# Gate tiles of the input projection moved from the branch stage in between the pieces of attention

## The chip, the cores and the metric

One core of one Trainium2 chip runs one program. The metric is the device time in microseconds; every number is for both layers and both token streams together. The program has one launch and no host arithmetic.

## The reference, cut to what matters

Two layers, one after the other, act on 1024 latent tokens and 128 prompt tokens (1152 in all, width 1024). In each, `h` is a modulated RMS norm of `x`, and one projection `h @ w_in` feeds three mixers and all their gates:

- the first is two gated long convolutions (by transforms), `y_hy`; the second differential attention in 4 heads, `y_at`; the third pooling, `y_pl`;
- each `y` is multiplied by `silu(z)` of its own 512 columns of the projection;
- `merged = sum over branches of sigmoid(mg_b) * (y_b @ w_b_o)`, `mg_b` being 1024 further columns each;
- `x + gate * (merged @ w_out)` is the next `x`.

Attention: per head two maps of queries and keys, `softmax` of each, `pr0 - lam * pr1`, times the values, then an RMS norm over the 128 value columns. Latent queries see 1024 latent and 256 cached keys, prompt queries the 128 prompt keys.

## The kernel before, in words

All tensors are held with channels (or tokens, for probabilities) on the 128 partitions. A product in fp32 is made of three in a rounded format: each operand is split into a rounded high part and a remainder, `hh`/`hl` for `h` and `wh`/`wl` for a weight tile. ScalarE rounds (`high`), GpSimd or VectorE subtracts (`low`), and TensorE forms high x high, high x low and low x high. A tile of 128 output columns over the 1152 tokens is 8 rows (k) x 3 products x 3 chunks of 384 columns, 72 matmuls; a branch product has 4 rows, 36 matmuls (`project`, line 120 on, whose matmul is L127).

The stages of a layer, each closed by a barrier, are: the filter network and spectra, `modulated_norm`, `mixers_in` (24 tiles of the projection), `values`, `long_conv` twice, `attention`, `branches_out`, `output`. The norm stores `hh` and `hl` to DRAM (`h_keep`, L612 and L614), since the convolutions need the room, and attention's ScalarE queue loads them again (4608 KB each). `values` loads `v` (2304 KB, L1055) for the first convolution, whose folds (L1323) start at once.

`attention` (L1394 on) runs 4 heads of 9 units: 8 blocks of 128 latent queries and one of prompt queries. Per unit, the two maps of scores (L1547) lie in two sets of three banks; VectorE takes the largest (L1840), ScalarE the exponential (L1683) and the scaling of the second map (L1690), GpSimd adds the maps (L1778); TensorE transposes the result in three fills of one bank (L1570), each of which ScalarE rounds (L1699) and VectorE takes the remainder of (L1860) before the next fill; every two units follow the product with the values (L1587), the sums of squares (L1596) and the spread of the root (L1604). The order in each engine's queue is written out by hand, unit u+1's scores between unit u-1's transposes.

`branches_out` (L1927 on) makes, for each of 3 branches, 4 gate tiles (12 in all, silu, L2041), splits `y * silu(z)` (L2083, L2046, L2085), and then 8 times a gate tile (24 in all, sigmoid, L2027) followed by a product of 4 rows, which VectorE multiplies by the gate (L2092) and adds to `merged` (L2097). The 36 gate tiles are those that the change moves. Weights come over SP's queue (L1959, L1963) into two buffers, are rounded by ScalarE (L2021) and subtracted by GpSimd (L2061), two tiles ahead:

```python
with pe.Fori(0, KD // 2) as i:
    for b in range(2):
...
        project(pe, chunks(banks(0)), wh[:, b], wl[:, b], hh, hl, KD).then_inc(S["g"], 1)
...
        project(pe, chunks(banks(1)), wh[:, b, KD:KO], wl[:, b, KD:KO], yh, yl, CT
                ).then_inc(S["z"], 1)
```

## Time and profile before

| | |
|---|---|
| median of 3 runs | 4578.84 us (4577.19 to 4579.85) |
| profiled execution, its span | 4593.8 us |
| mean granted TensorE clock | 0.886 |
| TensorE busy | 3727.9 us, 81% |
| VectorE, ScalarE, GpSimd busy | 36%, 27%, 26% |
| DMA | 428.99 MB, mean 93 GB/s |

The span is from the first to the last instruction of one profiled execution; the profile lists no other time for it. Times of an execution are in us from its start. A granted clock of 1.00 is 2.4 GHz, of 0.50 is 1.2 GHz. PE is TensorE, PEld its weight loads, DVE VectorE, ACT ScalarE, POOL GpSimd, SPq the queue of SyncE that issues DMAs.

### The profile page before, as it was taken

How to read it: one execution, taken by the hardware profiler on the slowest of the kernel's cores; microseconds unless marked ns; L12 is line 12 of the kernel's file. 1: busy time of each engine (PE TensorE's matmuls, PEld its weight loads, DVE VectorE, ACT ScalarE, POOL GpSimd, SP SyncE). 2: the span in 40 equal slices, each digit the busy share in tenths (PEclk: the TensorE clock that was granted, in tenths of full speed). 3: DMA queues.
4: the chain of work that ended last, by engine and by line, in shares of the span. 5: the costliest groups of instructions: out<-in, count | busy, mean ns of one | idle time of the engine just before them, and what ended most of it. 6: DMA issues, size and time to landing. Idle time of an engine off the chain costs nothing. (4 is left out here: it accounts for less than half of the span.)

```text
span 4593.8 us, 53336 instructions
## 1 busy us (share of the span) xinstructions
PE 3727.9 (81%) x19468; PEld 3375.5 (73%) x19468; DVE 1665.4 (36%) x1950; ACT 1256.8 (27%) x1848; POOL 1175.2 (26%) x542
## 2 busy tenths in 40 slices
PE   3874999787577799999938849997875777999998
PEld 2664988565466699999926649885664567999998
DVE  4234323254666412121242343232546664121212
ACT  2232122122455412121122321221224563121211
POOL 2011121054343222212120121210543342212211
PEclk8877999888787899999968779998887888999999
DMA  2544211234511111110415442122445111111104
GB/s 85 185 132 182 87 64 71 93 128 160 173 36 45 46 54 65 34 68 30 141 54 185 135 180 87 63 78 88 134 157 167 37 44 53 51 62 37 64 32 149
DMA packets 156156, 428.99 MB, mean 93 GB/s; under 512 B 30202, under 2 KB 51966, under 8 KB 154688
## 3 DMA queue, kind: packets, MB, share of 16 engines
q1 hardware_dynamic: 139936, 379.55, 24.8%
q10 hardware_dynamic: 16128, 48.26, 2.9%
q8 instruction: 52, 0.85, 0.1%
q14 instruction: 40, 0.33, 0.0%
HBM read 312.38 MB, written 120.08 MB: 94 GB/s over the span
## 5 line engine op out<-in xcount | busy, mean ns | idle before, releaser
L2061 POOL TENSOR_TENSOR branch_wl<-branch_raw,branch_wh 128x1536 fp32r<-128x1536 f32 (+1 forms) x72 | 267.3, 3713 | 926.5 <-ACT branch_wh L2021 926.5
L127 PE MATMUL ps<-hh,branch_wh 128*128 128x384 f32 x1728 | 398.2, 338 | 41.2 <-POOL branch_wl L2061 24.2
L127 PE MATMUL ps<-hl,branch_wh 128*128 128x384 f32 x1728 | 396.2, 337 | 0.0
L127 PE MATMUL ps<-hh,branch_wl 128*128 128x384 f32 x1728 | 396.1, 337 | 0.0
L127 PEld LDWEIGHTS ps<-hh,branch_wh 128*128 128x128 f32 x1728 | 311.5, 190 | 44.5 <-issue 44.5
L2092 DVE TENSOR_TENSOR branch_gate<-ps,branch_gate 128x1152 f32<-128x1152 f32 x48 | 65.2, 1358 | 751.8 <-PE ps L127 751.8
L127 PEld LDWEIGHTS ps<-hl,branch_wh 128*128 128x128 f32 x1728 | 311.9, 190 | 0.0
L127 PEld LDWEIGHTS ps<-hh,branch_wl 128*128 128x128 f32 x1728 | 311.5, 190 | 0.0
L1292 POOL TENSOR_TENSOR conv_dl<-conv_draw,conv_dh 128x512 fp32r<-128x512 f32 x128 | 180.2, 1415 | 471.4 <-ACT conv_dh L1242 470.6
L1778 POOL TENSOR_TENSOR attn_prob<-attn_prob 128x1280 f32<-128x1280 f32 (+1 forms) x72 | 190.4, 2644 | 241.1 <-ACT attn_prob L1690 241.1
L127 PE MATMUL ps<-hh,mixin_wh 128*128 128x384 f32 x720 | 167.2, 340 | 102.2 <-POOL mixin_wl L943 97.0
L1840 DVE TENSOR_REDUCE attn_nmax<-ps 128x1 f32<-128x1280 f32 x144 | 194.7, 1353 | 43.9 <-PE ps L1547 43.7
L127 PEld LDWEIGHTS ps<-hh,mixin_wh 128*128 128x128 f32 x720 | 130.4, 191 | 106.6 <-issue 98.2
L1570 PE MATMUL ps<-ident,attn_prob 128*128 128x128 f32 x648 | 125.6, 313 | 101.1 <-DVE attn_wl L1860 100.6
L943 POOL TENSOR_TENSOR mixin_wl<-w_in_raw,mixin_wh 128x1024 fp32r<-128x1024 f32 x48 | 114.7, 2392 | 350.9 <-ACT mixin_wh L868 350.9
L2021 ACT CAST branch_wh<-branch_raw 128x1536 fp32r<-128x1536 f32 (+1 forms) x72 | 96.2, 1339 | 382.2 <-PE ps L127 382.1
L2027 ACT ACTIVATE branch_gate<-ps 128x1152 f32<-128x1152 f32 x48 | 54.5, 1135 | 524.8 <-PE ps L127 524.8
L1683 ACT ACTIVATE attn_prob<-ps,attn_nmax 128x1280 f32<-128x1280 f32 x144 | 176.1, 1223 | 68.3 <-DVE attn_nmax L1840 63.9
L868 ACT CAST mixin_wh<-w_in_raw 128x1024 fp32r<-128x1024 f32 x48 | 50.2, 1049 | 489.2 <-DMA w_in_raw<-in_w_in 371.2
L1570 PEld LDWEIGHTS ps<-ident,attn_prob 128*128 128x128 f32 x648 | 83.5, 159 | 127.4 <-DVE attn_wl L1860 93.6
L1547 PE MATMUL ps<-attn_kh,attn_qs 128*128 128x512 f32 (+2 forms) x400 | 133.6, 446 | 44.7 <-DVE attn_kl L1832 34.7
L127 PE MATMUL ps<-hl,mixin_wh 128*128 128x384 f32 x720 | 165.9, 338 | 0.0
(262 smaller groups left out, 8421.2 us busy)
## 6 DMA issues: line engine op xcount, KB each, us to landing
branch_raw<-in_w_mo SPq DMA_DIRECT2D x48, 768.0 KB, 4.2
H_dram<-fspec_hout ACTq DMA_DIRECT2D x100, 256.0 KB
fspec_araw<-in_w_ada SPq DMA_DIRECT2D x48, 512.0 KB, 4.6
conv_hs<-H_dram SPq DMA_DIRECT2D x32, 768.0 KB, 4.5
w_in_raw<-in_w_in SPq DMA_DIRECT2D x44, 512.0 KB, 3.8
fspec_draw<-in_dft_taps SPq DMA_DIRECT2D x68, 256.0 KB, 3.0
conv_draw<-in_dft_fwd SPq DMA_DIRECT2D x64, 256.0 KB, 2.6
conv_draw<-in_dft_inv SPq DMA_DIRECT2D x64, 256.0 KB, 2.6
```

Source lines behind the costliest of these rows:

```text
L127: last = pe.matmul(out, w[:, k, :], x[:, k, cols], start=(k == 0 and n == 0), stop=(k == kt - 1 and n == 2))
L943: pool.tensor_tensor(wl[:, b], raw[:, b], wh[:, b].bitcast(F32), ALU.subtract).then_inc(S["lo"], 1)
L1292: pool.tensor_tensor(dl[:, b], draw[:, b], dh[:, b].bitcast(F32), ALU.subtract).then_inc(S["lo"], 1)
L1547: last = pe.matmul(flat[:, 1536 * c + at:1536 * c + at + width], qs[:, c, q0:q0 + P], keys[:, c, k0 + at:k0 + at + width], start=(m == 0), ...
L1570: last = pe.transpose(ps[:, 6, q * P:(q + 1) * P], prob0[:, u % 3, (at + q) * P:(at + q + 1) * P], ident[:])
L1683: nc.scalar.activation(dst[:, 0:n], flat[:, 1536 * c:1536 * c + n], ACT.Exp, bias=nmax[:, c:c + 1], accum_out=total[:, u % 2, c:c + 1]).th ...
L1778: pool.tensor_tensor(prob0[:, u % 3, 0:n], prob0[:, u % 3, 0:n], prob1[:, u % 2, 0:n], ALU.add).then_inc(S["w"], 1)
L1840: dve.tensor_reduce(nmax[:, c:c + 1], flat[:, 1536 * c:1536 * c + n], AX_X, ALU.max, negate=True).then_inc(S["max"], 1)
L2021: nc.scalar.copy(wh[:, b, 0:size], raw[:, b, 0:size]).then_inc(S["hi"], 1)
L2027: nc.scalar.activation(three(gate[:, b]), banks(0)[:, :, 0:CH], ACT.Sigmoid).then_inc(S["sig"], 1)
L2061: pool.tensor_tensor(wl[:, b, 0:size], raw[:, b, 0:size], wh[:, b, 0:size].bitcast(F32), ALU.subtract).then_inc(S["lo"], 1)
L2092: dve.tensor_tensor(three(gate[:, b]), banks(1)[:, :, 0:CH], three(gate[:, b]), ALU.mult).then_inc(S["p"], 1)
```

## The change

The norm no longer stores `h`. Attention follows `values` directly, so `hh` and `hl` stay in place, and the convolutions come after it. `attention_and_gates` has 36 steps and 4 that drain; step n makes one gate tile, its 8 rows laid between the pieces of unit n (scores) and unit n-2 (transposes). The scores of both maps now share one set of three banks, `gate_banks` is another set of three; the probabilities of the second map and the split weights of the product with the values have one buffer where they had two. Gate weights come in half tiles (256 KB) into a ring of 3; ScalarE copies each finished tile out of its banks (`gate_out`), and SP stores it to `gates` in DRAM (576 KB), unactivated. The loops over heads are unrolled, as are those over the convolutions and the branches. `values` no longer loads `v`; the first convolution does, and waits for it. `branches_out` keeps only the 24 products: it loads each gate row (576 KB) and applies silu or sigmoid there, with weights (256 KB) in a ring of 3 and two buffers of gates; the first branch writes `merged` directly.

```diff
@@ build
             with ExitStack() as hctx:
...
-                raw = hctx.enter_context(nc.sbuf_tensor("w_in_raw", [P, 2, KD, P], F32))
-                modulated_norm(nc, A, l, ps, pr, mod, ones, x_state, hh, hl, raw, h_keep, s_kept)
-                wv = hctx.enter_context(nc.sbuf_tensor("w_v_raw", [P, KD, BR], F32))
-                mixers_in(nc, A, l, ps, pr, ident, hh, hl, raw, wv, mix, qk)
-                values(nc, A, O, l, ps, hh, hl, wv, mix, v, vrows, s_kept)
-            with nc.Fori(0, 2) as o:
-                long_conv(nc, A, l, o, ps, ident, v, mix, H_dram, Hp_dram, hinv)
-            vctx.close()
-            with ExitStack() as hctx:
-                hh = hctx.enter_context(nc.sbuf_tensor("hh2", [P, KD, NT], F32R))
-                hl = hctx.enter_context(nc.sbuf_tensor("hl2", [P, KD, NT], F32R))
-                attention(nc, A, O, l, ps, pr, ident, ones, qk, vrows, mix, hh, hl, h_keep)
...
-                branches_out(nc, A, l, ps, hh, hl, mix, merged, wo)
+                graw = hctx.enter_context(nc.sbuf_tensor("w_g_raw", [P, 3, KD // 2, P], F32))
+                with ExitStack() as wctx:
...
+                    values(nc, A, O, l, ps, hh, hl, wv, vrows, graw)
+                attention_and_gates(nc, A, O, l, ps, pr, ident, ones, qk, vrows, mix, gates, hh, hl, graw)
+            with ExitStack() as vctx:
...
+                for o in range(2):
+                    long_conv(nc, A, l, o, ps, ident, v, mix, H_dram, Hp_dram, hinv)
+            with ExitStack() as mctx:
...
+                branches_out(nc, A, l, ps, mix, gates, merged, wo)
@@ modulated_norm, sync
-                    sp.dma_start(h_keep[0, :, k], hh[:, k].bitcast(F32)).then_inc(s_kept, 16)
...
-                    sp.dma_start(h_keep[1, :, k], hl[:, k].bitcast(F32)).then_inc(s_kept, 16)
@@ values, sync
-                sp.dma_start(v[:], mix[2].rearrange("c p n -> p c n")).then_inc(s_hy, 16)
+                for j in range(3):
+                    sp.dma_start(graw[:, j], A["w_g"][l, j].rearrange("p (k c) -> p k c", c=P)).then_inc(s_gw, 16)
@@ long_conv, sync, then vector
+                if o == 0:
+                    sp.dma_start(v[:], mix[2].rearrange("c p n -> p c n")).then_inc(S["vin"], 16)
...
+                if o == 0:
+                    dve.wait_ge(S["vin"], 16)
@@ attention_and_gates, sync (step n is unit n = 9 h + u; NALL = 36, STEPS = 40)
+                for n in range(STEPS):
+                    if 1 <= n <= NALL:
+                        sp.wait_ge(S["gev"], n)
+                        sp.dma_start(gates[n - 1], stage[:]).then_inc(S["gst"], 16)
+                    gate_weights(2 * n + 5)
...
+                    gate_weights(2 * n + 6)
@@ tensor
+                def gate(n, *rows):
...
+                    for k in rows:
+                        if k == 0 and n:
+                            pe.wait_ge(S["gev"], n)
+                        j = 2 * n + k // HALF
+                        if k % HALF == 0:
+                            pe.wait_ge(S["glo"], j + 1)
+                        for m, (a, b) in enumerate(((gh, hh), (gh, hl), (gl, hh))):
+                            for c in range(3):
+                                last = pe.matmul(gate_banks[:, c, :], a[:, j % RING, k % HALF, :],
...
+                turn_cached(0)
+                turn_new(0)
+                for n in range(STEPS):
+                    if n == 0:
+                        gate(n, 0, 1, 2, 3)
+                    if n < NALL:
+                        scores(n, 0)
+                    gate(n, *((4, 5) if n == 0 else (0,)))
...
+                        spread(*got)
+                    if n:
+                        gate(n, 1)
+                    if got := due(n, WITH_V):
+                        with_v(*got)
...
+                        gate(n, 2)
+                    if n < NALL:
+                        scores(n, 1)
...
+                        turn(n - 2, 0)
+                    if n:
+                        gate(n, 3)
...
+                        sums(*got)
+                    if n:
+                        gate(n, 4)
+                    if len(turned) > 1:
+                        turn(n - 2, 1)
+                    if n:
+                        gate(n, 5)
+                    gate(n, 6)
+                    if len(turned) > 2:
+                        turn(n - 2, 2)
+                    gate(n, 7)
@@ scalar
+                for n in range(STEPS):
+                    if 1 <= n <= NALL:
+                        gate_out(n - 1)
+                        second_map(n - 1)
+                    if n < NALL:
+                        softmax(n, 0)
...
+                    gate_high(2 * n + 2)
+                    if got := due(n, WITH_V):
+                        take(*got)
...
+                        high(n - 2, 0)
+                    if n < NALL:
+                        softmax(n, 1)
+                    if len(turned) > 1:
+                        high(n - 2, 1)
+                    gate_high(2 * n + 3)
+                    if len(turned) > 2:
+                        high(n - 2, 2)
@@ branches_out, sync (NP = 24 products, q = 8 br + m; RING = 3)
+                def branch_in(br):
                     for t in range(CT):
+                        if br:
+                            sp.wait_ge(S["yl"], CT * (br - 1) + t + 1)
+                        sp.dma_start(z[:, t], gates[CT * br + t]).then_inc(s_z[t], 16)
+                        sp.dma_start(yin[:, t], mix[br + 4, t]).then_inc(s_z[t], 16)
+
+                def product_in(q):
+                    if q >= RING:
+                        sp.wait_ge(S["lo"], q - RING + 1)
+                    sp.dma_start(raw[:, q % RING], A["w_mo"][l, q // KD, q % KD]).then_inc(s_w[q % RING], 16)
+                    if q >= 2:
+                        sp.wait_ge(S["t"], q - 1)
+                    sp.dma_start(gate[:, q % 2], gates[N_BRANCH * CT + q]).then_inc(s_r[q % 2], 16)
+
+                branch_in(0)
+                for q in range(NP):
+                    product_in(q)
+                    if q % KD == 1 and q // KD + 1 < N_BRANCH:
+                        branch_in(q // KD + 1)
@@ tensor
+                for q in range(NP):
...
+                    pe.wait_ge(S["lo"], q + 1)
+                    if q >= 2:
+                        pe.wait_ge(S["p"], q - 1)
...
+                    project(pe, chunks(banks(q)), wh[:, q % RING], wl[:, q % RING], yh[:, br % 2], yl[:, br % 2], CT, ready
@@ scalar
+                silu(0)
+                for t in range(CT):
+                    round_y(0, t)
+                    if t < 2:
+                        high(t)
+                for q in range(NP):
+                    br, m = divmod(q, KD)
+                    high(q + 2)
+                    sigmoid(q)
+                    if br + 1 < N_BRANCH:
+                        if m == 2:
+                            silu(br + 1)
+                        elif 3 <= m < 3 + CT:
+                            round_y(br + 1, m - 3)
@@ vector
+                for q in range(NP):
+                    br, m = divmod(q, KD)
+                    if br + 1 < N_BRANCH and 3 <= m < 3 + CT:
+                        gated(br + 1, m - 3)
+                    dve.wait_ge(S["sig"], q + 1)
+                    dve.wait_ge(S["mm"], q + 1)
+                    if br == 0:
+                        dve.tensor_tensor(three(merged[:, m]), banks(q)[:, :, 0:CH], three(gate[:, q % 2]), ALU.mult
...
+                    else:
...
+                        dve.tensor_tensor(merged[:, m], merged[:, m], gate[:, q % 2], ALU.add).then_inc(S["t"], 1)
```

## Rows read from the trace of the kernel before

**Rows 1.** The page of the profile, its first line
```profile
span 4593.8 us, 53336 instructions
```

**Rows 2.** Windows: attention and branches, layer 0, then layer 1; columns as in the header
```profile
core 0: us, PE busy (x) PEld busy (x) DVE busy (x) ACT busy (x) POOL busy (x), PEclk, DMA share, GB/s
1187.77:1564.20 376.43, 255.80 (x1386) 216.77 (x1386) 231.85 (x345) 207.62 (x342) 140.76 (x64) 0.79 0.24 68
1564.20:2192.35 628.15, 606.98 (x3456) 605.25 (x3456) 127.24 (x73) 121.48 (x100) 133.62 (x36) 0.98 0.16 53
...
3478.49:3849.16 370.67, 252.76 (x1386) 214.44 (x1386) 232.42 (x345) 207.41 (x342) 140.79 (x64) 0.81 0.24 69
3849.16:4476.61 627.45, 606.31 (x3456) 604.59 (x3456) 127.30 (x73) 121.48 (x100) 133.66 (x36) 0.98 0.16 53
```

**Rows 3.** Timeline, start of attention, layer 0: start us, us, engine, line, operation, tiles
```profile
1187.77 2.46 SPq L1482 DMA_DIRECT2D attn_qraw<-qk  x4
...
1202.11 1.09 PE L1534 MATMUL ps<-ident,attn_craw 128*128 128x128 f32 x4 [13.00 <-DMA attn_craw<-in_cache_k]
...
1204.11 0.58 ACT L1669 CAST attn_kh<-ps 128x512 fp32r<-128x512 f32 x1
...
1209.38 0.68 DVE L1832 TENSOR_TENSOR attn_kl<-ps,attn_kh 128x512 fp32r<-128x512 f32 x1
```

**Rows 4.** Timeline, branches of layer 0: matmuls of the first tile, two sigmoids later
```profile
1574.03 1.16 PE L127 MATMUL ps<-hl,branch_wh 128*128 128x384 f32 x3
...
1574.99 1.16 PE L127 MATMUL ps<-hh,branch_wl 128*128 128x384 f32 x3
...
1660.78 1.14 ACT L2027 ACTIVATE branch_gate<-ps 128x1152 f32<-128x1152 f32 x1 [10.99 <-PE ps L127]
...
1679.50 1.14 ACT L2027 ACTIVATE branch_gate<-ps 128x1152 f32<-128x1152 f32 x1 [9.69 <-PE ps L127]
```

**Rows 5.** Timeline, TensorE's weight loads within a unit of attention
```profile
1336.22 0.19 PEld L1587 LDWEIGHTS ps<-attn_wh,attn_vh 128*128 128x128 f32 x1
...
1338.00 0.54 PEld L1547 LDWEIGHTS ps<-attn_kh,attn_qs 128*128 128x128 f32 x3
...
1339.16 0.47 PEld L1570 LDWEIGHTS ps<-ident,attn_prob 128*128 128x128 f32 x4
```

**Rows 6.** Timeline, the end of attention, layer 0
```profile
1546.90 0.55 PE L1587 MATMUL ps<-attn_wh,attn_vh 128*128 128x256 f32 x1 [1.16 <-DVE attn_y L1876]
...
1560.85 0.35 DVE L1876 SCALAR_TENSOR_TENSOR attn_y<-attn_og,attn_gain,ps 128x128 f32<-128x128 f32 x1 [1.52 <-PE ps L1604]
```

**Rows 7.** DMA issues: KB each, median us to landing; last, landing of norm_x by tile
```profile
hyena_v<-mix SPq DMA_DIRECT2D x2, 2304.0 KB, 8.7
...
branch_yin<-mix SPq DMA_DIRECT2D x24, 576.0 KB, 3.8
...
conv_draw<-in_dft_fwd SPq DMA_DIRECT2D x64, 256.0 KB, 2.6
...
w_out_raw<-in_w_out SPq DMA_DIRECT2D x12, 512.0 KB, 5.2
...
DMA to landing us min/median/max: 3.7/7.0/10.1
```

**Rows 8.** Groups by line, whole span: busy us, mean ns | idle before
```profile
L1242 ACT CAST conv_dh<-conv_draw 128x512 fp32r<-128x512 f32 x128 | 77.9, 621 | 310.6 <-PE ps L1201 113.8 <-PE ps L1232 106.2 <-DMA conv_draw<-in_dft_fwd 69.5
...
L632 ACT ACTIVATE norm_sq<-norm_x 128x1152 f32<-128x1152 f32 x16 | 18.6, 1163 | 28.1 <-DMA norm_x<-x_state 15.1 <-PE ps L622 13.1
...
L2092 DVE TENSOR_TENSOR branch_gate<-ps,branch_gate 128x1152 f32<-128x1152 f32 x48 | 65.2, 1358 | 751.8 <-PE ps L127 751.8
...
L2027 ACT ACT_TABLE_LOAD x18 | 23.1, 1283 | 10.3 <-DVE branch_yl L2085 10.1
```

**Rows 9.** Groups by line and shape, window of attention, layer 0
```profile
L1840 DVE TENSOR_REDUCE attn_nmax<-ps 128x1 f32<-128x1280 f32 x64 | 95.1, 1487 | 22.5 <-PE ps L1547 22.5
...
L1683 ACT ACTIVATE attn_prob<-ps,attn_nmax 128x1280 f32<-128x1280 f32 x64 | 85.1, 1330 | 35.6 <-DVE attn_nmax L1840 33.4
...
L1570 PE MATMUL ps<-ident,attn_prob 128*128 128x128 f32 x324 | 63.2, 315 | 51.8 <-DVE attn_wl L1860 51.6
```

More of the change, by code:

```diff
@@ L1063, in _ @@
                 sp.wait_ge(s_st[1], 16 * 5)
-                sp.wait_ge(s_hy, 16)
+                sp.wait_ge(s_gw, 48)
             @block.scalar
@@ L1406, in attention @@
     G = 2
-    UNITS = [(u, u * P, 0, KEYS) for u in range(QT)] + [(QT, TS, KEYS, TP)]
+    NU, NPV = QT + 1, QT // G + 1
+    NALL, STEPS = HEADS * NU, HEADS * NU + 4
+    HALF = KD // 2
+    RING = 3
     with phase(nc, "attn") as ph:
@@ new lines, in scores, with turn @@
+                    for m, keys in enumerate((kh, kl)):
+                        for at in range(0, width, 512):
+                            size = min(512, width - at)
+                            last = pe.matmul(flat[:, at:at + size], qs[:, c, q0:q0 + P],
+                                             keys[:, c, k0 + at:k0 + at + size], start=(m == 0), stop=(m == 1))
+                    last.then_inc(S["s"], 1)
+                def turn(n, f):
+                    if f == 0:
+                        pe.wait_ge(S["w"], n + 1)
+                        pe.wait_ge(S["nk"], 1 + min(HEADS - 1, (n + 3) // NU))
+                    at, cnt = fills(n)[f]
+                    if filled(n, f):
+                        pe.wait_ge(S["wl"], filled(n, f))
@@ L1701, in high @@
+                def high(n, f):
+                    act.wait_ge(S["tr"], filled(n, f) + 1)
+                    at, cnt = fills(n)[f]
+                    h, u = divmod(n, NU)
+                    before = NPV * h + u // G
+                    if f == 0 and (u % G == 0 or u == QT) and before:
+                        act.wait_ge(S["pv"], before)
+                    nc.scalar.copy(weights(wh, n, at, cnt), ps[:, 6, 0:cnt * P].rearrange("p (k c) -> p k c", c=P)
                                    ).then_inc(S["wh"], 1)
@@ L1914, in _ @@
[L1914 to L1940 removed]
+                sample_queries(0)
@@ new lines, in _ @@
+                cached_keys(0)
+                prompt(0)
+                for n in range(STEPS):
+                    if 1 <= n <= NALL:
+                        scales(n - 1)
+                    if n < NALL:
+                        maximum(n, 0)
+                    if (h := coming(n, 8)) is not None:
+                        cached_keys(h)
+                    if got := due(n, SPREAD):
+                        scale(*got)
+                    if n < NALL:
+                        maximum(n, 1)
+                    turned = fills(n - 2) if 2 <= n < NALL + 2 else []
+                    if turned:
+                        low(n - 2, 0)
+                    if got := due(n, WITH_V):
+                        means(*got)
+                    if len(turned) > 1:
+                        low(n - 2, 1)
+                    if len(turned) > 2:
+                        low(n - 2, 2)
+                    if (h := coming(n, 7)) is not None:
+                        sample_queries(h)
+                    if (h := coming(n, 8)) is not None:
+                        prompt(h)
@@ new lines, in round_y, with sigmoid @@
+                def round_y(br, t):
+                    act.wait_ge(S["gated"], CT * br + t + 1)
+                    if br >= 2 and t == 0:
+                        act.wait_ge(S["mm"], KD * (br - 1))
+                    nc.scalar.copy(yh[:, br % 2, t], z[:, t]).then_inc(S["yh"], 1)
+                def sigmoid(q):
+                    act.wait_ge(s_r[q % 2], 16 * (q // 2 + 1))
+                    nc.scalar.activation(gate[:, q % 2], gate[:, q % 2], ACT.Sigmoid).then_inc(S["sig"], 1)
+                silu(0)
```

742 lines of the change are left out of this document (298 added, 444 removed).

## The prediction, made before the changed kernel was run

> **What bounds the kernel now.** I read the stages by windows first, then the steady stretches in the timeline, then the sizes of transfers and of single operations. The profiled execution has a span of 4593.8 us [rows 1]; the median of the runs is 4578.84 us, 15.0 us (0.3%) less, so I work out a difference and take it off the median. The windows [rows 2] run from the first DMA of a stage to that of the next. Attention takes 376.4 and 370.7 us in the two layers, with TensorE busy for 256 and 253 us at a mean granted clock of 0.79 and 0.81; the branches take 628.2 and 627.5 us with TensorE busy 97% at 0.98. Together 2002.7 us of the span. The branches are bound by TensorE, attention by chains of waits between engines; that difference is what the change works on.
>
> **Unit prices.** From one sigmoid of a branch to the next lie 108 matmuls of 384 columns (72 of a gate tile, 36 of a product), and 18.72 us [rows 4]: 0.1733 us each at the full level (2.4 GHz), no loss between tiles. At the lower level (1.2 GHz) three take 0.96 us, so 0.32 each [rows 4]. A gate tile is then 12.48 us, a product 6.24. In attention [rows 5] a map's scores take 1.16 us (1338.00 to 1339.16), 15 matmuls with the values 1.78 us (1336.22 to 1338.00), four 128-column transposes 0.47.
>
> **Attention with gates.** A full unit costs TensorE two maps 2.33, ten transposes 1.15 and a gate tile 12.48: 15.96 us, x32 = 510.7. With the values: 16 x 3.57 = 57.1. Sums and spreads, four small matmuls each, I take at the price of four transposes, 0.5: 16.0. The four short prompt steps are 14.1 each (gate tile and 1.6 of small work): 56.4; key turning 2.4. Sum 642.6. Of this 6.2 runs in the start and 6.8 in the tail, leaving 629.6.
> Waits: one has no cover. The gate tile has one set of banks, and row 0 of the next waits for ScalarE's copy (1.14 us, as the sigmoid's row [rows 4], and some 0.3 of pipeline and semaphore) while only one map's scores (1.16) stand ahead: 0.3 us in 32 steps and 1.2 in the four short ones, 14.4. The other waits are covered: the largest and the exponential need 1.49 + 1.33 us [rows 9], plus the copy and the scaling of the second map ahead of them, some 4.4 us from the step's start, and TensorE comes back for the second map after 6; a filled transpose bank needs about 2 us of ScalarE and VectorE, with 3.1 us of gate rows behind it. Per step ScalarE gains two casts of 0.62 [rows 8] and the 1.14 copy, GpSimd two remainders, on some 6 and 4 us they have now, against 18 of TensorE. DMA gains two loads of 256 KB and a store of 576 KB per 18 us, on SP, and a transfer of 576 KB lands in 3.8 us [rows 7], within a step. All at nothing.
> Start [rows 3]: loads land 14.3 us after the first issue (1187.8 to 1202.1). The prompt keys are now turned only after the cached keys' remainder: cast until 1204.7, 0.7 of VectorE, 0.5 to turn, 1205.9. Then 36 gate matmuls; the first tile of the branches begins at the lower level too, so I take 11 at 0.32 and 25 at 0.1733, 7.8: 25.9 in all. Tail: the last full unit's transposes go without gates between them, about 5; from its product with the values to the last scaling now 1546.9 to 1561.2 at mostly the lower level [rows 6], 14. Barrier 3.2 (to 1564.2, rows 2's boundary). Stage: 25.9 + 629.6 + 14.4 + 19 + 3.2 = 692.1 us. Lower bound without the 14.4: 678. Upper bound with a further 0.5 us of waits per step: 710.
>
> **Branches without gates.** TensorE's share is 24 x 6.24 = 150 us per layer, but I do not take that as the stage's time. SP issues for product q: weights, then (after the addition of q-2) the gate; the weights of q+1 stand behind that wait. ScalarE's order is round(q+2), then sigmoid(q). So sigmoid(i) waits for weights(i+2), these for the wait ahead of gate(i+1), and that for addition(i-1): a ring through four engines, once per product. Price: 0.25 us from VectorE to SP's issue; gate (576 KB) and weights (256 KB) landing one behind the other; round 0.62; sigmoid 1.16; multiply 1.36; add 1.36, taken as the multiply's [rows 8]; 0.25 of semaphores. The pair's landing isn't in the trace. Eight 576 KB loads issued together land from 3.7 to 13.8 us after the first issue (the last has 10.1, issued 3.6 later), so 1.44 us per further 576 KB [rows 7]: 3.7 + 0.64 = 4.35. Bounds: 256 KB alone (2.6) behind an issue of 0.5, 3.1; and the 5.2 of weights behind two 576 KB stores [rows 7]. I take 4.35 since its row is the same kind of load. The ring is 9.33 us in branches 1 and 2, 7.9 in branch 0 (no addition), and 2.75 more in the four steps that also split the next branch's y (ScalarE round 1.16, VectorE remainder 1.36), with one 1.3 us table load where silu gives way to sigmoid [rows 8]. All above TensorE's 6.24.
> Start: eight loads (4.7 MB) land by 13.8; four silus are first on ScalarE, so the first y tile is split at 17.6, the next each 4.0 later (round, remainder, multiply alternate): 29.6. Weights(2) stand behind the second branch's first loads and land at 35.7; the first addition ends at 40.3. Branch 0 to 107.9 (three more of 7.9, four of 10.65, one table load). There the third branch's 4.7 MB stand ahead of weights(10): nine 576 KB and 256 KB, 15.9 instead of 4.35, so product 8 ends at 128.9. Then two steps of 9.33 (147.5), one of 13.4, three of 12.1, one of 9.33 (206.5), eight of 9.33: 281.2, and 1.1 of barrier: 282.3 us. Bounds: the pair's landing at 3.1 takes 26 off, at 5.2 adds 19. With idle gaps of 3 us the clock may fall as it does in attention now; at the lower level throughout a product is 11.5, which would add 41.
> The Trainium skill, "DMA: Bandwidth & Descriptors", Bandwidth, prices a transfer at 2.0 us plus its bytes over 436 GB/s. By it the pair would land in 3.95 us, an estimate, and the stage would be 9 us shorter; the eight loads here (1.44 us per 590 kB, 2.3 fixed) lie near it.
>
> **The rest.** v (2304 KB) was loaded under the values stage; now the first convolution's folds wait for it: 8.7 us landing [rows 7], +8.6 a layer. The convolutions' other loads queue behind it, but the transposes they serve come later still. The 16 stores of h per layer, its two loads of 4608 KB and the clearing of merged go; the first two were hidden under the norm, mixer and attention stages, and the last under the wait for the branches' first weights, so nothing beyond what the windows hold. Unrolling the loops: bounded by zero and a few us, taken as 0.
>
> **Sum.** After: 2 x (692.1 + 282.3) + 17.2 = 1966.0, against 2002.7: 36.7 us less. 4578.84 - 36.7 = **4542 us**, 0.8% less. Its own range: attention -28 to +36, branches -52 to +82 for both layers; not all at once: 4490 to 4600.
>
> **Rivals.**
> 1. *Slower: attention's chains surface.* TensorE's queue is in order, so a late transpose bank now also holds back gate rows. Before a transpose it idles 51.8 us per layer now [rows 9], 1.6 a unit. If gate rows hid none of this and each step kept 1.5 us, 72 steps add 108: 4650 us. It decides from 0.51 us a step (36.7/72). Against it stand 3.1 us of rows between each transpose and the next, against a chain of 2. Chance 0.20.
> 2. *The branches keep TensorE busy.* If the ring isn't there (loads land far earlier than reckoned, or the waits are already met), the stage is 32.5 to the first product's end, 23 x 6.24 = 143.5 and 5 at its end: 181, so 202 less: 4340 us. Against it: the order is written out in the code. Chance 0.10.
> 3. *The change doesn't interleave.* If gate rows only lengthen the present steps, attention takes 376 + 449 and the stages 2 x 133 more: 4808 us. Against it: the work was idle time of TensorE (120 us per stage) and a low clock. Chance 0.05.
>
> **How the numbers follow.** A measurement of this kernel can tell about 0.2% (9 us) from no change. The forecast has 0.65. Its spread around -37 us puts some 0.49 of all beyond -9, 0.08 within 9 and 0.08 slower. With rival 2: faster 0.59; same 0.10 with a little of rival 1; slower 0.31. Range 4470 to 4640: it leaves out rivals 2 and 3 and about half of the first.
>
> **What would show it.** Right: windows of the attention stage near 692 us at a clock of 0.95 or more, TensorE's idle time before gate row 0 near 0.3 us a step and named ScalarE's copy; a branch stage near 282 us with TensorE busy some 55%, ScalarE's round waiting on the weights' DMA, additions 9.3 us apart in branch 2, and a stall of some 12 us at product 10. Wrong: products 6.2 us apart (rival 2), idle before transposes of over 0.5 us a step (rival 1), a clock near 0.8 in attention, or folds of the first convolution starting at once.

## The result, and the profile after

| | before | after |
|---|---|---|
| median, first set of runs | 4578.01 us (4 runs) | 4505.62 us (4 runs, 4499.88 to 4511.35) |
| ratio | | 0.9841, 95% interval 0.9825 to 0.9858 |
| the same kernels, a later set | 4585.11 us (9 runs) | 4525.41 us (4 runs), ratio 0.9865, interval 0.9841 to 0.9889 |
| TensorE busy, mean clock of the profiled execution | 3727.9 us, 0.886 | 3681.1 us, 0.895 |

The kernel is faster by 72 us in the first set of runs and by 60 us in the second; the forecast was 36.7. The profiled execution of after, whose own time is 4511.35 us, answers to [rows 1] with

```profile
span 4509.7 us, 51806 instructions
```

The windows of attention and of the branches, in both layers, answer to [rows 2]:

```profile
core 0: us, PE busy (x) PEld busy (x) DVE busy (x) ACT busy (x) POOL busy (x), PEclk, DMA share, GB/s
...
884.70:1582.80 698.10, 660.16 (x3978) 633.93 (x3978) 247.78 (x349) 292.83 (x450) 240.55 (x136) 0.98 0.27 80
...
1884.10:2146.50 262.40, 183.51 (x864) 175.70 (x864) 87.63 (x64) 74.74 (x79) 32.22 (x24) 0.82 0.38 136
...
3131.50:3829.10 697.60, 659.61 (x3978) 633.37 (x3978) 247.73 (x349) 292.81 (x450) 240.56 (x136) 0.98 0.26 80
4131.50:4395.10 263.60, 177.33 (x864) 169.20 (x864) 87.63 (x64) 74.80 (x79) 32.09 (x24) 0.84 0.38 136
```

Attention with the gates takes 698.1 and 697.6 us, TensorE busy 95% at a clock of 0.98 where it had 0.79 and 0.81. The branches take 262.4 and 263.6, TensorE busy 70% and 67% at 0.82 and 0.84. By stages, both layers, windows between the first issues of the stages:

| us | before | forecast | after | before again | after again |
|---|---|---|---|---|---|
| attention (and gates) | 747.1 | 1384.2 | 1395.7 | 744.9 | 1396.6 |
| branches | 1255.6 | 564.6 | 526.0 | 1255.7 | 535.3 |
| convolutions | 590.1 | 607.3 | 603.7 | 579.5 | 604.1 |
| mixers | 814.2 | 814.2 | 801.0 | 805.4 | 806.2 |
| whole span | 4593.8 | 4557.1 | 4509.7 | 4572.3 | 4530.7 |

The last two columns are further executions, from the experiments. They show what one execution can tell: the two spans of before lie 21.5 us apart and those of after 21.0, so the difference of the first pair (84.1) and of the second (41.6) both miss the medians' 60 to 72. Stage by stage the two pairs agree within 3 us on attention and on the branches of before; they lie 9 us apart on the branches of after and 11 on the convolutions of before.

**The pace of the branches.** One turn in the third branch, from the timeline of layer 0 (start, duration, engine, line, tiles, in brackets the idle time before and what ended it):

```profile
2109.39 1.36 DVE L2079 TENSOR_TENSOR merged<-merged,branch_gate 128x1152 f32<-128x1152 f32 x1
2110.77 0.33 SPq L1980 DMA_DIRECT2D branch_gate<-gates  x1
2111.28 0.34 SPq L1977 DMA_DIRECT2D branch_raw<-in_w_mo  x1
2114.93 0.62 ACT L2013 CAST branch_wh<-branch_raw 128x512 fp32r<-128x512 f32 x1 [6.96 <-DMA branch_raw<-in_w_mo]
2115.45 1.16 ACT L2029 ACTIVATE branch_gate<-branch_gate 128x1152 f32<-128x1152 f32 x1
...
2116.65 1.36 DVE L2076 TENSOR_TENSOR branch_gate<-ps,branch_gate 128x1152 f32<-128x1152 f32 x1 [5.90 <-ACT branch_gate L2029]
2118.04 1.36 DVE L2079 TENSOR_TENSOR merged<-merged,branch_gate 128x1152 f32<-128x1152 f32 x1
2119.42 0.33 SPq L1980 DMA_DIRECT2D branch_gate<-gates  x1
```

The addition ends at 2110.75, SP's wait is met and the gate goes out at 2110.77, the weights behind it at 2111.28. They are there for the rounding at 2114.93, whose idle time before, 6.96 us, is named the weights' DMA. Sigmoid 0.52 later, multiply 1.20 after that, addition 1.39 after that. This is the ring that the prediction drew. This turn takes 8.65 us (2110.77 to 2119.42) and is the shortest of six; the other additions of the third branch, up to product 21, begin at

```profile
2082.65 1.36 DVE L2079 TENSOR_TENSOR merged<-merged,branch_gate 128x1152 f32<-128x1152 f32 x1
2091.69 1.36 DVE L2079 TENSOR_TENSOR merged<-merged,branch_gate 128x1152 f32<-128x1152 f32 x1
...
2100.64 1.36 DVE L2079 TENSOR_TENSOR merged<-merged,branch_gate 128x1152 f32<-128x1152 f32 x1
...
2126.92 1.36 DVE L2079 TENSOR_TENSOR merged<-merged,branch_gate 128x1152 f32<-128x1152 f32 x1
```

(the first of these is product 15). The turns are 9.04, 8.95, 8.75, 8.65, 8.88 and 8.93 us, 8.87 on average, and differ by the landing of the pair, which takes 4.16 to 4.55 us from the gate's issue to the rounding; all the rest of a turn is 4.5 us each time.

The last two products of the layer:

```profile
2133.26 2.21 ACT L2029 ACTIVATE branch_gate<-branch_gate 128x1152 f32<-128x1152 f32 x2
...
2135.85 1.36 DVE L2079 TENSOR_TENSOR merged<-merged,branch_gate 128x1152 f32<-128x1152 f32 x1
...
2138.51 1.36 DVE L2079 TENSOR_TENSOR merged<-merged,branch_gate 128x1152 f32<-128x1152 f32 x1
2140.89 1.17 ACT L2029 ACTIVATE branch_gate<-branch_gate 128x1152 f32<-128x1152 f32 x1 [5.42 <-DMA branch_gate<-gates]
2142.55 1.36 DVE L2076 TENSOR_TENSOR branch_gate<-ps,branch_gate 128x1152 f32<-128x1152 f32 x1 [2.68 <-PE ps L127]
2143.95 1.36 DVE L2079 TENSOR_TENSOR merged<-merged,branch_gate 128x1152 f32<-128x1152 f32 x1
```

Additions end at 2137.21, 2139.87 and 2145.31: 2.66 and 5.44 us apart. Where product 10's weights stand behind the third branch's eight loads:

```profile
1990.47 0.33 SPq L1980 DMA_DIRECT2D branch_gate<-gates  x1
1990.84 0.43 SPq L1971 DMA_DIRECT2D branch_z<-gates  x1
...
1994.92 0.60 SPq L1977 DMA_DIRECT2D branch_raw<-in_w_mo  x1
2006.67 0.62 ACT L2013 CAST branch_wh<-branch_raw 128x512 fp32r<-128x512 f32 x1 [17.68 <-DMA branch_raw<-in_w_mo]
...
2009.78 1.36 DVE L2079 TENSOR_TENSOR merged<-merged,branch_gate 128x1152 f32<-128x1152 f32 x1
```

From the gate's issue to the rounding 16.2 us pass instead of some 4.4; ScalarE idles 17.68.

**Attention.** From the list of waits of layer 0's stage (us in total, times, longest), three lines:

```profile
PEld ps L1634 <- ACT attn_stage L1751: 17.6, 35, 1.7
...
PE ps L1634 <- ACT attn_stage L1751: 5.6, 4, 1.5
...
PE ps L1590 <- DVE attn_wl L1896: 3.2, 2, 1.8
```

The idle time before transposes, 51.8 us in [rows 9], is 3.2. What is left is gate row 0, which waits for ScalarE's copy of the last tile. The first two lines name it. For the matmuls it is 5.6 us in four waits, one in each short prompt step (1.4 us on average, forecast 1.2). For the weight loads (PEld) it is 17.6 us in 35, but those overlap with work: in a full step the row starts 0.2 us late, as the timeline shows.

```profile
1193.28 0.74 PE L1577 MATMUL ps<-attn_kl,attn_qs 128*128 128x512 f32 x3
1194.07 0.79 PE L1634 MATMUL ps<-hh,attn_gh 128*128 128x384 f32 x3
1194.70 0.68 PE L1634 MATMUL ps<-hl,attn_gh 128*128 128x384 f32 x3
1195.22 0.69 PE L1634 MATMUL ps<-hh,attn_gl 128*128 128x384 f32 x3
```

The gate row (second line) begins 0.79 us after three score matmuls that fill 0.58, as the three ahead of them did. Its own first three then take 0.63 to the next line, the following three 0.52.

### The profile page after: what moved, and what is told of

It is laid out like the page before. It is cut to its first block and busy times, and to the rows that moved or that the text cites. A ratio compares the mean times of both kernels' runs of the same rounds, so it can differ in the third digit from the quotient of the medians.

```text
span 4509.7 us, 51806 instructions
## 1 busy us (share of the span) xinstructions
PE 3681.1 (82%) x19468; PEld 3343.2 (74%) x19468; DVE 1613.9 (36%) x1940; ACT 1333.8 (30%) x2022; POOL 1173.2 (26%) x662
## 5 line engine op out<-in xcount | busy, mean ns | idle before, releaser
L1634 PE MATMUL ps<-hh,attn_gh 128*128 128x384 f32 x1728 | 428.3, 356 | 13.9 <-ACT attn_stage L1751 11.2
L1634 PE MATMUL ps<-hl,attn_gh 128*128 128x384 f32 x1728 | 396.5, 337 | 0.0
L1634 PE MATMUL ps<-hh,attn_gl 128*128 128x384 f32 x1728 | 394.4, 335 | 0.0
L1800 POOL TENSOR_TENSOR attn_gl<-w_g_raw,attn_gh 128x512 fp32r<-128x512 f32 x144 | 185.7, 1290 | 528.2 <-ACT attn_gh L1689 528.0
L1634 PEld LDWEIGHTS ps<-hh,attn_gh 128*128 128x128 f32 x1728 | 287.3, 190 | 36.0 <-ACT attn_stage L1751 35.1
L1634 PEld LDWEIGHTS ps<-hl,attn_gh 128*128 128x128 f32 x1728 | 311.9, 189 | 0.0
L1634 PEld LDWEIGHTS ps<-hh,attn_gl 128*128 128x128 f32 x1728 | 310.1, 188 | 0.0
L127 PE MATMUL ps<-branch_yh,branch_wh 128*128 128x384 f32 x576 | 154.7, 381 | 183.0 <-DVE branch_gate L2076 74.1
L127 PEld LDWEIGHTS ps<-branch_yh,branch_wh 128*128 128x128 f32 x576 | 115.8, 217 | 199.2 <-issue 125.5
L1896 DVE TENSOR_TENSOR attn_wl<-ps,attn_wh 128x512 fp32r<-128x512 f32 (+2 forms) x200 | 117.5, 587 | 336.2 <-ACT attn_wh L1736 336.2
```

What stands on the lines that cost most here:

```text
L127: last = pe.matmul(out, w[:, k, :], x[:, k, cols], start=(k == 0 and n == 0), stop=(k == kt - 1 and n == 2))
L1634: last = pe.matmul(gate_banks[:, c, :], a[:, j % RING, k % HALF, :], b[:, k, c * CH:(c + 1) * CH], start=(k == 0 and m == 0), stop=(k == K ...
L1800: pool.tensor_tensor(gl[:, j % RING], graw[:, j % RING], gh[:, j % RING].bitcast(F32), ALU.subtract).then_inc(S["glo"], 1)
L1896: dve.tensor_tensor(weights(wl, n, at, cnt), ps[:, 6, 0:cnt * P].rearrange("p (k c) -> p k c", c=P), weights(wh, n, at, cnt).bitcast(F32), ...
```

## The experiments

Eleven runs, in three sets, each set on one chip with its own runs of the kernel before (medians 4592, 4591 and 4585 us), so ratios are what compares across sets.

**1. The kernel before, profiled once more.** No edit.

> The kernel before, unchanged, profiled once more. The mixers' stage got 7.3 and 5.9 us shorter in the two layers, which I had put at nothing. If the change causes this (its 16 stores of h per layer gone, tiles at other places in memory), the stage takes 406.9 and 407.3 us again, within 1 us. If it is only how this one execution went, it comes out between 400 and 405, and the span near the median of 4578 instead of 4593.8.

Span 4572.3 us. Its window of the mixers in layer 0:

```profile
426.88:829.60 402.72, 372.82 (x2088) 355.01 (x2088) 124.21 (x117) 76.82 (x108) 78.28 (x32) 0.95 0.23 81
```

402.7 us, and the same in layer 1, where the first execution had 406.9 and 407.3, with the stores of `h` in place. The changed kernel profiled again (experiment 11) has 403.3 and 403.0, without them. So the 13 us in the first pair are how those executions went. TensorE's busy time, the same 2088 matmuls, moves with it, 371 to 377 us over the runs read.

**2. ScalarE's order turned.**

```diff
-                    high(q + 2)
                     sigmoid(q)
+                    high(q + 2)
```

> ScalarE takes the sigmoid of product q ahead of the rounding of the weights of q+2; nothing else is changed. Theory (a ring through ScalarE's order and SP's order sets the pace of the branches, 8.6 to 9.0 us a product): the ring is open, TensorE sets the pace, products 6.2 to 7 us apart; product 2 still waits for weights that land 37.6 us into the stage, so the stage takes 180 to 200 us instead of 262, and the kernel is some 140 us faster than the changed one, near 4365 us. Rival (the DMAs of the stage themselves, 832 KB a product, or VectorE's work set the pace): the stage stays within 5 us of 262 and the kernel at 4506.

Ratio to before 0.9642 (0.9613 to 0.9672), 4423.26 us. The window of the branches, layer 0:

```profile
1892.23:2108.42 216.19, 166.00 (x864) 161.15 (x864) 90.67 (x64) 74.76 (x79) 35.45 (x24) 0.87 0.47 166
```

216 us instead of 262, so the ring is what held them; in the third branch products are 6.24 us apart from its third on. But the stage is above my 180 to 200: in the first two branches ten steps of 8.8 to 14.0 us remain. There `high(q + 2)`, which still waits for weights issued behind the gate (110.1 us of ScalarE's idle time name their DMA), stands ahead of the rounding of the next branch's y, and VectorE's remainder of y ahead of its multiply. So the cause of the longer steps is read from the order in the code and from that wait; no run takes it apart. I had taken the last branch's pace for the whole.

**3. Weights ahead of the wait on SP.** The same ring opened at its other end; ScalarE's order is that of the change.

```diff
-                    if q >= RING:
-                        sp.wait_ge(S["lo"], q - RING + 1)
-                    sp.dma_start(raw[:, q % RING], ...)
                     if q >= 2:
                         sp.wait_ge(S["t"], q - 1)
                     sp.dma_start(gate[:, q % 2], ...)
+                    weights_in(q + 2)
```

(`weights_in` holds the two lines that are taken out; the weights of products 0 and 1 go out ahead of the loop)

> SP issues the weights of product q+2 behind the gate of product q, so ahead of the wait for the addition of q-1; ScalarE's order stays as it is. The same ring is opened at its other end. Theory: products 6.2 to 7 us apart as in the run with the sigmoid first, and the start is shorter too, since the weights of product 2 stand ahead of the second branch's loads: first addition ends near 36 us instead of 43; stage 175 to 195 us, kernel near 4355 us. Rival (transfers or VectorE set the pace): stage within 5 us of 262, kernel near 4506.

Ratio 0.9527 (0.9499 to 0.9556), 4373.99 us. The window of the stage, and two multiplies in a row of the third branch:

```profile
1892.39:2082.31 189.92, 157.43 (x864) 154.44 (x864) 93.86 (x64) 75.27 (x79) 36.22 (x24) 0.90 0.53 189
...
2065.83 1.36 DVE L2083 TENSOR_TENSOR branch_gate<-ps,branch_gate 128x1152 f32<-128x1152 f32 x1 [3.49 <-PE ps L127]
...
2072.07 1.36 DVE L2083 TENSOR_TENSOR branch_gate<-ps,branch_gate 128x1152 f32<-128x1152 f32 x1 [3.49 <-PE ps L127]
```

189.9 us, in the range of the theory. The multiplies are 6.24 us apart and wait for TensorE's matmuls, no longer for ScalarE: TensorE sets the pace, as rival 2 priced it. The rival of this run, transfers or VectorE as the bound, falls: the same bytes go through in 72 us less.

**4. Attention's new order without the gate tiles' work.** Left out are the gate weights, their roundings and remainders, the 36 tiles' matmuls and the copies; the gates become the constant 0.5. The 36 stores stay.

```diff
                 def gate(n, *rows):
+                    return
...
                 def gate_out(n):
+                    return
```

> The attention stage keeps its new order and its 36 stores of a tile, but the gate tiles' weights, roundings, remainders, matmuls and copies are left out, so the gates are a constant 0.5. Theory (the gate tiles fill TensorE's idle time and lift its clock, the order alone is worth little): the stage takes 350 to 380 us at a granted clock near 0.8, as attention did before (376 and 371), so 449 us of gate tiles cost 320 to 350. Rival (the new order of attention by itself is quicker): stage under 330. Rival (attention's waits surfaced in the new order): stage over 400. The branch stage stays at 262.

The windows of the mixers in layer 1, then of attention in layer 0:

```profile
2498.89:2909.96 411.07, 376.38 (x2088) 356.55 (x2088) 125.14 (x117) 76.84 (x109) 78.20 (x32) 0.94 0.22 78
...
891.25:1401.00 509.75, 310.27 (x1386) 259.96 (x1386) 239.32 (x350) 217.18 (x342) 147.28 (x64) 0.67 0.24 74
```

509.75 us at a clock of 0.67, the third of my three cases: without its filling the new order is 133 to 136 us slower in layer 0 than attention was before (376.4 and 374.0 in its two executions). TensorE waits 87.5 us before transposes and 64.5 before scores. By its own chains a step takes 14.2 us (509.75 / 36, with start and tail), against 19.4 (698.1 / 36) once the gate rows are in. What lies between, some 5 us, is an estimate of the margin against rival 1; no run narrows it down to the point where the chains surface.

**5. The same with two sets of score banks.**

```diff
-                            last = pe.matmul(flat[:, at:at + size], qs[...],
+                            last = pe.matmul(flat[:, 1536 * c + at:1536 * c + at + size], qs[...],
...
-                        pe.wait_ge(S["exp"], 2 * n + c)
+                        pe.wait_ge(S["exp"], 2 * n + c - 1)
```

> As the run without gate work (gates a constant 0.5), but each of the two maps has its own three score banks again, as in the kernel before; the gate tiles had taken the second set. That run's attention stage took 510 us, not the 350 to 380 I expected. Theory (with one set of banks the scores of a map wait for the exponential of the other, and this chain is what costs 134 us more than attention did before): the stage falls to 380 to 430 us. Rival (the single prob1 and weight buffers, or the order of the pieces, carry it): it stays above 470.

```profile
888.41:1337.10 448.69, 279.62 (x1386) 240.44 (x1386) 238.04 (x350) 214.78 (x342) 147.47 (x64) 0.75 0.27 84
```

448.7 us, between theory and rival: the banks that the gates took carry 61 of the 136 us against the 374.0 of experiment 1. The other 75, over single buffers for the second map and the split weights, the order itself and the lower clock (0.75 against 0.79), were not divided further.

**6. The branches' loads spread, on top of 3.**

```diff
-                    if q % KD == 1 and q // KD + 1 < N_BRANCH:
-                        branch_in(q // KD + 1)
+                    if q % KD < CT and q // KD + 1 < N_BRANCH:
+                        branch_in(q // KD + 1, [q % KD])
```

> On top of the weights issued ahead: the next branch's eight loads no longer go out together behind product 1 of a branch, but two behind each of its products 0 to 3, with the silus one product later. Theory (4.7 MB in one go hold up the gate and weights of product 10 by some 5 to 9 us in the open ring): no addition more than 7.5 us behind the last, stage 180 to 184 us instead of 189.9 and 188.2, kernel 10 to 18 us below the 4374 of the weights ahead. Rival (the same bytes cost the same wherever they stand): stage within 2 us of 189.

Ratio 0.9493 (0.9472 to 0.9514), 4359.06 us; the stage takes 185.5 and 183.7 us, 4.4 and 4.5 less. The kernel's 15 us less come in part from other stages, and the two kernels ran on different chips. The size is at the low end: in experiment 3 two additions came 11.2 and 10.9 us behind the ones before them. With the loads spread the first takes TensorE's 6.2; the other, with the silus in it, moves one product on and still takes 9.4.

**7. The start woven, on top of 6.**

```diff
-                silu(0)
+                silu(0, [0])
                 for t in range(CT):
+                    if t + 1 < CT:
+                        silu(0, [t + 1])
                     round_y(0, t)
-                    if t < 2:
-                        high(t)
+                    if t >= 2:
+                        high(t - 2)
```

> On top of the spread loads: at the start of the branches ScalarE rounds each y tile behind the next silu instead of behind all four. Theory (the start is a chain of silu, multiply, round and remainder, on view in rows as 32 us to the last remainder, of which loads take only 15): the first product is added 25 to 28 us into the stage instead of 35.5; stage 170 to 176 us, kernel another 14 to 20 us down, near 4340. Rival (the start is bound by the loads of z and y, and then by the first weights behind them): under 3 us a layer.

Ratio 0.9462 (0.9442 to 0.9482), 4341.73 us, the fastest kernel of the study. The stage:

```profile
1881.49:2060.40 178.91, 152.44 (x864) 151.51 (x864) 91.82 (x64) 75.18 (x79) 36.09 (x24) 0.93 0.57 200
```

178.9 and 177.5 us, 6.4 less a layer, under the forecast of 8 to 14; the first addition ends at 30.6 us, not 25 to 28, with the splits of y still 3.8 to 4.9 apart. TensorE is now busy for 152 of 179 us; 20.7 of its 26.5 idle us lie in the first 22.9, ahead of the first product.

**8. The third fill behind gate row 7**, on the changed kernel.

```diff
                     gate(n, 6)
-                    if len(turned) > 2:
-                        turn(n - 2, 2)
                     gate(n, 7)
+                    if len(turned) > 2:
+                        turn(n - 2, 2)
```

(and its rounding behind ScalarE's copy of the next step, its remainder behind VectorE's scales there)

> The changed kernel with one piece of attention moved: the third transpose fill of a unit stands behind gate row 7 instead of ahead of it, so 0.23 us more work covers ScalarE's copy of the gate tile. Theory (that copy is the only wait left in attention, 0.2 us a step): the attention stage falls from 698 to 692 us, kernel 10 to 14 us below the changed one's 4506. Rival (ScalarE's queue then holds the copy or the second map back behind the late cast, and the wait moves): attention stays at 698 or rises to 705.

Attention is slower, 707.7 and 708.2 us. For the whole kernel the ratio is 0.9872 (0.9853 to 0.9892), which overlaps with both intervals of the changed one. The theory's gain is there: from copy to copy 32 of the 35 steps are 0 to 0.7 us shorter. But the three steps that turn the cached keys of the next head take 26 to 27 us instead of 21.6. Among what ended TensorE's idle time before those transposes (us, times) is

```profile
  DVE attn_wl L1897: 13.0, 3
```

where the changed kernel has nothing but the first load: the key turning shares the transposes' bank and waits for the late fill, three times a stage.

**9. The same, except in the step ahead of a key turning.** The edit adds `and n % NU != 7` to the condition.

> The changed kernel with the third fill behind gate row 7, except in the step ahead of a head's key turning. In the run before, 31 of 35 steps were shorter by 0 to 0.7 us, but the one step a head boundary that turns the cached keys grew by 4.4 to 5.4 us, since those wait for the late fill. Theory (that wait alone turned a gain of some 6 us a layer into a loss of 10): the attention stage takes 690 to 694 us, the kernel 8 to 16 us less than the changed one on the same chip. Rival (VectorE's and ScalarE's queues lose elsewhere what the copy gains): attention 697 us or more.

Attention takes 694.7 and 694.6 us, 3.5 and 3.8 below the changed kernel on the same chip (698.2 and 698.4). Ratio 0.9858 (0.9837 to 0.9880) against 0.9865 (0.9841 to 0.9889) for the changed one: the stage gained what the rows show, the whole kernel no more than can be told.

**10. Parts 3, 6, 7 and 9 together.**

> Everything that paid, together: weights ahead, loads spread, start woven, third fill behind row 7 except before the key turning. If the parts are independent, branches 178 us and attention 692 us a layer, and the time is that of the run with the woven start (ratio 0.9462 to before) less 12 us: ratio 0.9436, near 4320 us where before is 4578. Rival (attention's gain does not hold): ratio 0.9462 again.

Ratio 0.9480 (0.9463 to 0.9498), 4344.41 us, short of the 0.9436 of the theory. Branches 177.3 and 177.1, attention 694.8 and 695.4, as the parts had them, yet not below the 0.9462 of experiment 7. Its convolutions took 606.8 us together, those of experiment 7 591.7. Mixers, the same code in all runs, differ by as much (801 to 818 us for both layers); the two kernels are not told apart.

**11. The changed kernel again.**

> The changed kernel unchanged, on the chip and in the rounds of the two others. If the mixers' 7 us a layer were only the scatter of one execution, its mixer stages come out anywhere between 399 and 411 us as in the other runs, and the ratio to before lies inside 0.9825 to 0.9858; if the chips differ in more than their level, outside.

Ratio 0.9865 (0.9841 to 0.9889), its centre just outside the first interval; mixers 403.3 and 403.0 us. The branches take 268.2 and 267.1, 4 to 6 more than in the first execution. Its plain turns (those that do not also split the next branch's y) are 9.19 us on average in layer 0 and 9.03 in layer 1, against 8.88 and 8.98. One of them takes 10.4 and 10.0 us, since its pair lands 5.9 and 5.5 us after the issue; layer 1 of the first execution has such a turn too, layer 0 has none. And the last step takes 7.0 us in both layers instead of 5.4 and 5.5: a part of the last product runs at the lower level of the clock, three matmuls in 0.96 us, and the last multiply waits for it.

## Why the prediction was off, and where it was right

The direction, the likeliest case, the ring and the one uncovered wait of attention held, and the time lies in the range; the gain is 60 to 72 us instead of 37. The second pair of executions, 41.6 us apart, would have made the forecast look right, but by luck: in it the branches gain 29 us more than forecast, and attention and the convolutions take 22 of them back.

**The step that failed: "Then two steps of 9.33 (147.5), one of 13.4, three of 12.1, one of 9.33 (206.5), eight of 9.33: 281.2".** The stage came out 19.9 us below its 282.3 in layer 0. The last two of the eight are 8.1 us instead of 18.7: for q of 22 and 23 `high(q + 2)` does nothing, so the sigmoid has no weights to wait for and the ring is broken where the products end. That is in the code that I read, and I ran the ring through to the last product; it is 10.6 of the 19.9 (9.0 in the second set, where the last step is 7.0).

Most of the other 9.3 is the price of a turn. The nine plain turns behind product 8 take 8.60 to 9.04, 8.88 on average, instead of 9.33: 4.1 us. The landing is not to blame: 4.38 in these turns, 4.35 forecast. The rest of a turn is 4.5 instead of 5.0: in the rows above 0.52 from rounding to sigmoid (0.62), 1.20 and 1.39 as reckoned, and the two terms of 0.25 for hand-overs, which take 0.02 to 0.04 each (the gate's issue follows the addition's end by 0.02). No row stood behind those two terms. The eight steps that also split the next y take 6.9 us less than forecast in all; a part of it is again the ring, and a part the 2.75 that I added, whose two named terms (1.16 and 1.36) make 2.52. The first addition, 1.8 us late, takes some of this back.

**The rest of the branches.** First addition's end 42.1 against 40.3 (the splits are 4.9, 4.9 and 3.8 us apart, not 4.0). Branch 0 ends at 106.3 (forecast 107.9), product 8 at 127.0 (128.9): the stall behind 4.7 MB of loads was reckoned at 15.9 us from issue to rounding and is 16.2. TensorE is busy 70% and 67% of the stage, not 55: at a clock of 0.82 and 0.84 part of the products run at the lower level.

The Trainium skill, "DMA: Bandwidth & Descriptors", Anatomy of one DMA — SWDGE (gpsimd) path, gives the 2.0 us plus bytes over 436 GB/s that the prediction quoted, as a fit for transfers issued by GpSimd; the prediction named the section on bandwidth and left that condition out, and the loads here are issued by SyncE. The 3.95 us that it gives for the pair is an estimate. The traces do not bear it out: 4.0 to 4.7 us in the first execution's layer 0, 4.4 on average, against the row-based 4.35. With 3.95 the stage's forecast would have been 9 us nearer, but for a wrong reason, since the error lies in the end of the ring and in the hand-overs.

**Attention.** Forecast 692.1, measured 698.1 and 697.6. The scores of the first unit begin 27.6 us into the stage (25.9 forecast), the tail with the barrier takes 21.6 (22.2), so the middle carries the rest: 648.9 us against 644.0. (In the tail [rows 6] give 14.3 and 3.0 where I wrote 14 and 3.2, which changes nothing.) The wait for the copy is 0.2 us in the timeline where I had 0.3. In its place, matmuls of a gate row that follow another kind of work take 0.60 to 0.63 for the first three instead of 0.52, five to six times a step, which the sum had at nothing: some 18 us a stage, an estimate from these rows. Four transposes take 0.35 instead of the 0.47 of [rows 5], some 10 us less, and the waits for the copy 2 less, so that 5 to 6 are left, as measured. "No loss between tiles" holds within a run of one kind only. Experiment 9 moved 0.23 us of cover in some 30 steps, 7 us, and got 3.6 a layer.

**Convolutions.** Forecast +17.2 us in both layers, measured +13.6 and, in the second pair, +24.6 (before alone varied by 10.6). What the wait costs is clearer in the rows. The first convolution of the changed kernel:

```profile
1582.80 0.40 SPq L1134 DMA_DIRECT2D hyena_v<-mix  x1
...
1591.41 2.29 DVE L1319 TENSOR_TENSOR conv_fold<-hyena_v 128x2048 f32<-128x2048 f32 x1 [11.15 <-DMA hyena_v<-mix]
...
1593.76 1.97 PE L1175 MATMUL ps<-ident,conv_fold 128*128 128x128 f32 x8 [13.88 <-DVE conv_fold L1319]
1594.85 1.28 ACT L1236 CAST conv_dh<-conv_draw 128x512 fp32r<-128x512 f32 x2 [17.18 <-DMA conv_draw<-in_dft_fwd]
...
1596.04 1.07 ACT L1243 CAST conv_xh<-ps 128x512 fp32r<-128x512 f32 x2
...
1607.09 3.75 PE L1181 MATMUL ps<-conv_xp,conv_dp 128*128 128x512 f32 x4 [0.78 <-ACT conv_xp L1243]
```

and of the kernel before (experiment 1):

```profile
886.83 0.36 SPq L1141 DMA_DIRECT2D conv_hp<-Hp_dram  x1
...
889.22 1.97 PE L1181 MATMUL ps<-ident,conv_fold 128*128 128x128 f32 x8 [6.80 <-DVE conv_fold L1323]
...
893.10 1.29 ACT L1242 CAST conv_dh<-conv_draw 128x512 fp32r<-128x512 f32 x2 [10.06 <-DMA conv_draw<-in_dft_fwd]
...
894.29 1.07 ACT L1249 CAST conv_xh<-ps 128x512 fp32r<-128x512 f32 x2
...
905.35 3.75 PE L1187 MATMUL ps<-conv_xp,conv_dp 128*128 128x512 f32 x4 [0.78 <-ACT conv_xp L1249]
```

The folds start 8.61 us after the stage's first issue (8.7 by [rows 7]) and the first transposes 10.96 us after it instead of 2.39. By the prompt's product the delay is 24.3 - 18.5 = 5.8 us. In both kernels ScalarE rounds the first `conv_draw` before it takes the first transposes, and that rounding, whose wait is named the DMA, starts 12.05 us into the stage instead of 6.27: the same 5.8 us. So what delays the stage is `conv_draw`, whose load now stands behind v, and not the folds, whose later start it covers. The prediction had the wait for the folds right, but took it for the cost, and set the loads queued behind v at nothing.

**The rest, at 0.** The mixers' 13 us less would have been the largest miss after the branches. Experiments 1, 4 and 11 show it as scatter: 399.5 to 411.1 us over the same 2088 matmuls.

**Rival 1** did not happen: idle time before transposes 3.2 us, not 51.8. The prediction set the cover (3.1 us of gate rows) against a chain of 2, fill by fill. By experiment 4 a whole step has 14.2 us of chain, at the clock of that run, against 19.4 with the gate rows. Gate tiles of 449 us therefore cost 188 us against the new order without them and 324 against attention as it was; the forecast of 318 was against the second. **Rival 2** was priced at 181 us for its stage; experiments 3 and 7 open the ring and give 189.9 and 178.9. **Rival 3** is out: the clock is 0.98 and the stage 698 us, not 825.

Nothing was tried for a second set of gate banks: all eight banks are in use.

## What to carry to other kernels

Before pricing a chain that repeats, look whether it is closed (a load issued behind a wait for the previous result, behind it in another engine's queue the very work that result needs), and then at its first and last turns, where a guard such as `q < NP` can open it. When a change gives a stage's idle time to other work, ask which queue the freed stage now leans on: here the gates' way through DRAM, new with the move, closed a ring, and opening it, with one reordered DMA issue, was worth some 150 us in two stages, twice what the move itself brought. And measure a filled stage once without its filling: it gives an estimate of the margin that is left.

## What the runs showed of the hardware

VectorE and GpSimd hold each other up. At the start of the branches a multiply of two tensors in memory takes 2.42 us where it takes 1.36 alone, and it is the one that begins while GpSimd's remainder runs:

```profile
1901.63 1.91 POOL L2050 TENSOR_TENSOR branch_wl<-branch_raw,branch_wh 128x512 fp32r<-128x512 f32 x1 [24.31 <-ACT branch_wh L2013]
...
1902.35 2.42 DVE L2057 TENSOR_TENSOR branch_z<-branch_z,branch_yin 128x1152 f32<-128x1152 f32 x1
```

GpSimd's instruction ends at 1903.54; from there to the multiply's end at 1904.77 lie 1.23 us, about a multiply. The multiply at 1912.18, with no remainder beside it, takes 1.35. The remainder itself takes 1.91 us where it takes 1.3 alone; it begins while VectorE's own remainder, 1901.07 to 1902.43, still runs. By the Trainium skill, "SBUF — State Buffer", SBUF: two separate sides, a VectorE instruction with two inputs in SBUF and a GpSimd instruction that reads SBUF take a shared port pair by an exclusive lock, and the other waits for the whole instruction; the rows agree. It is why two of the three splits of y were 4.9 us apart, where the one without a remainder beside it was 3.8.

And one execution says less about a stage than its neat rows suggest: the mixers, untouched, took between 399.5 and 411.1 us, and the spans of one kernel lay 21 us apart in two sets of runs, more than half of the gain that was forecast; a whole-kernel difference of 1% is read from repeated times, a stage's from its chain of rows.
